# Token sums moved to VectorE, transposes half a tile later, one load and some weight work reordered

## The reference, cut to what matters

```
hp = hp + mix_out(a_p, d_p, w_out)                                  # 1024 x 1024
hp = hp + swiglu(rms_norm(hp, norm_ffn_g), w_gate, w_up, w_down)    # D_FF = 2816
y  = rms_norm(hp, final_norm_g)

def swiglu(h, w_gate, w_up, w_down):
    g = einsum('bsd,df->bsf', h, w_gate)
    u = einsum('bsd,df->bsf', h, w_up)
    return einsum('bsf,fd->bsd', silu(g) * u, w_down)
```

## Time and profile before

| | |
|---|---|
| median of three runs | 2763.15 us |
| the profiled execution | 2758.85 us, span 2757.0 us |
| TensorE busy | 2566.0 us (93%) |
| VectorE busy | 1827.6 us (66%) |
| ScalarE busy | 1211.1 us (44%) |
| GpSimd busy | 602.7 us (22%) |

### The profile page before, as it was taken

One profiled execution on the slowest core, in us unless ns is written; L12 is line 12 of the kernel. 1 busy time (PEld: TensorE's weight loads), 2 busy tenths in 40 slices (PEclk: granted clock), 3 DMA queues, 4 the chain that ended last, 5 costly groups with the idle time before them and its releaser, 6 DMA issues.

```text
span 2757.0 us, 48148 instructions
## 1 busy us (share of the span) xinstructions
PE 2566.0 (93%) x19292; PEld 1592.7 (58%) x19292; DVE 1827.6 (66%) x3577; ACT 1211.1 (44%) x2108; POOL 602.7 (22%) x610
## 2 busy tenths in 40 slices
PE   3999999978899998887899999999889999999998
PEld 1666666656677766443344444444447777766666
DVE  8777776668878773666787788776554444444445
ACT  4566666657889997443232233223331111111112
POOL 1211111105667666122312111201120000000001
PEclk9999999988999999998999999999999999999999
DMA  5123211142210000523353334434212222222222
GB/s 183 56 73 107 95 59 66 46 110 49 40 32 9 9 9 9 191 108 138 130 184 115 115 133 175 151 122 149 105 39 69 70 79 87 88 77 69 70 74 76
DMA packets 149872, 245.81 MB, mean 89 GB/s; under 512 B 47298, under 2 KB 102002, under 8 KB 148114
## 3 DMA queue, kind: packets, MB, share of 16 engines
q1 hardware_dynamic: 149650, 242.74, 26.6%
HBM read 148.83 MB, written 90.94 MB: 87 GB/s over the span
## 4 chain that ended last, share of the span: by engine, by line
PE 50%; DVE 3%; issue 2%; POOL 2%; DMA 1%; ACT 1%; SPq 0%; POOLq 0%; DVEq 0%; ACTq 0%
PE bank L2843 10%; PE bank L2844 10%; PE bank L2845 10%; PE bank L2858 6%; PE bank L2860 5%; PE bank L2859 5%; PE bank L2795 1%; PE bank L2796 1%; PE bank L2797 1%; DMA tail_buffers<-mix_scratch 1%; PE bank L2778 1%; DVE tail_buffers L2216 1%; ACT tail_buffers L2567 0%; POOL tail_buffers L2102 0%; DMA out_y_prompt<-residual_rows 0%
## 5 line engine op out<-in xcount | busy, mean ns | idle before, releaser
L2843 PE MATMUL bank<-ffn_inT_sums,tail_buffers 128*128 128x512 f16 (+2 forms) x1848 | 579.8, 314 | 5.5 <-ACT tail_buffers L2605 3.0
L2844 PE MATMUL bank<-ffn_inT_sums,tail_buffers 128*128 128x512 f16 (+2 forms) x1848 | 579.4, 314 | 0.0
L2845 PE MATMUL bank<-ffn_inT_sums,tail_buffers 128*128 128x512 f16 (+2 forms) x1848 | 579.4, 314 | 0.0
L2342 DVE SCALAR_TENSOR_TENSOR residual_rows<-bank,pair_scales,residual_rows 128x512 f32<-128x512 f32 (+1 forms) x374 | 273.1, 747 | 114.7 <-PE bank L2860 114.3
L2858 PE MATMUL bank<-tail_buffers 128*128 128x512 f16 (+1 forms) x748 | 286.9, 384 | 20.3 <-issue 10.2
L1095 PE MATMUL z_ps<-w_in_hi_lo,normT_hi 128*128 128x384 f16 x816 | 268.4, 329 | 21.7 <-DVE w_in_hi_lo L682 21.7
L2859 PE MATMUL bank<-tail_buffers 128*128 128x512 f16 (+1 forms) x748 | 286.3, 383 | 0.0
L2860 PE MATMUL bank<-tail_buffers 128*128 128x512 f16 (+1 forms) x748 | 286.3, 383 | 0.0
L1096 PE MATMUL z_ps<-w_in_hi_lo,normT_hi 128*128 128x384 f16 x816 | 268.5, 329 | 0.0
L1097 PE MATMUL z_ps<-w_in_hi_lo,normT_lo 128*128 128x384 f16 x816 | 268.2, 329 | 0.0
L2843 PEld LDWEIGHTS bank<-ffn_inT_sums,tail_buffers 128*128 128x128 f16 x1848 | 181.3, 98 | 105.8 <-issue 5.6
(11 more groups left out here) (333 smaller groups left out, 5151.0 us busy)
## 6 DMA issues: line engine op xcount, KB each, us to landing
gate_up_scratch<-tail_buffers SPq DMA_DIRECT2D x77, 512.0 KB, 3.2
tail_buffers<-gate_up_scratch SPq DMA_DIRECT2D x77, 512.0 KB, 3.5
tail_buffers<-in_w_gate SPq DMA_DIRECT2D x22, 512.0 KB, 5.4
tail_buffers<-in_w_up SPq DMA_DIRECT2D x22, 512.0 KB, 6.5
tail_buffers<-in_w_down SPq DMA_DIRECT2D x22, 512.0 KB, 5.9
down_scratch<-tail_buffers SPq DMA_DIRECT2D x22, 512.0 KB, 3.1
tail_buffers<-down_scratch SPq DMA_DIRECT2D x22, 512.0 KB, 4.4
keys_values<-in_w_in SPq DMA_DIRECT2D x8, 1152.0 KB, 16.0
```

The source lines that it names most:

```text
L2342: nc.vector.scalar_tensor_tensor(out, BK[y_bank(e, y)][0:rows, :], PS[0:rows, i, F_YI:F_YI + 1], out, ALU.mult, ALU.add).then_inc(h_ok, 1)
L2843: nc.tensor.matmul(out, wh, nh, start=first and k == 0, stop=False, skip_group_check=True)
L2844: nc.tensor.matmul(out, wh, nl, start=False, stop=False, skip_group_check=True)
L2845: last = nc.tensor.matmul(out, wl, nh, start=False, stop=k == 3, skip_group_check=True)
```

## The change

1. The four differences of a unit are made by VectorE, in the tile in which the unit's second row is normalised, right behind `norm_row`; their order is now 0, 1, 2, 3.
2. The split of the 2048 columns is cut in two (`row_hi` and `row_lo` with m = 2 and 3), the second behind the tile's last batch of copies.
3. Every batch of transposes comes one half product later. Batch 0 of unit 3 stands in the middle of the second half product of tile 8; its batches 1 to 3, and batch 3 of unit 7 besides all of unit 8, stand between the first products of the FFN.
4. `load_mix(Q0 + 2)` (the third tile of the second half) is issued ahead of the last two loads of residual rows and of the loads of stored weights.
5. In pairs 0 and 1 of the first half, maxima, scales and slots of the next pair come earlier on VectorE and ScalarE, and slots 5 and 6 of pair 1 come later, at the start of pair 1.

```diff
 def turn_at(q, n):
-    u, m = norm_unit(q)
-    if q == 8:
-        return 3, n
-    if u in (0,):
+    k = 2 * q + n - 5 if q < Q0 else 2 * (q - Q0) + n + 15
+    if k < 0 or k == 15:
         return None
-    return (4 if u == 5 else u - 1), 2 * m + n
+    return k // 4, k % 4
...
+                load_mix(Q0 + 2)
                 load_rows(Q0 + 6)
                 load_rows(Q0 + 7)
                 for j in range(3):
                     slot_back(0, j)
                 down_back(0)
-                for q in range(Q0 + 2, NTT):
+                for q in range(Q0 + 3, NTT):
                     load_mix(q)
...
-                def token_sums(u):      # on GpSimd
...
+                def token_sums(u):      # on VectorE
...
+                    nc.vector.tensor_tensor(part(0), NF[1][:, half[0]], NF[0][:, half[0]], ALU.subtract).then_inc(t_ok, 1)
+                    dve.wait_ge(t_ok, 4 * u + 1)
+                    nc.vector.tensor_tensor(part(1), NF[1][:, half[1]], part(0), ALU.subtract).then_inc(t_ok, 1)
+                    nc.vector.tensor_tensor(part(2), NF[1][:, half[1]], NF[1][:, half[0]], ALU.subtract).then_inc(t_ok, 1)
+                    dve.wait_ge(t_ok, 4 * u + 2)
+                    nc.vector.tensor_tensor(part(3), NF[0][:, half[1]], part(1), ALU.subtract).then_inc(t_ok, 1)
...
# output_tile(q) on VectorE
                     elif q:
                         norm_row(q - 1)
+                        if norm_unit(q - 1)[1]:
+                            token_sums(norm_unit(q - 1)[0])
                         row_lo(*norm_unit(q - 1))
                     residual(q, 0)
...
+                    both = 4 if q == Q0 else norm_unit(q - 1)[0] if q and norm_unit(q - 1)[1] else None
+                    if both is not None:
+                        row_lo(both, 2)
+                    if q == Q0 - 1:
+                        turned_lo(3, 0)
                     residual(q, 1)
-                    if turn_at(q, 1):
+                    if turn_at(q, 1) and q != Q0 - 1:
                         turned_lo(*turn_at(q, 1))
+                    if both is not None:
+                        row_lo(both, 3)
...
# pairs 0 and 1 on VectorE, first half
+                    if i == 1:
+                        slot_lo(1, 5)
+                        slot_lo(1, 6)
                     if i:
                         max_down(i)
+                    if i == 1:
+                        max_gate_up(2, 0)
                     product_act(0, i, i, 512, 0)
...
+                    if i == 1:
+                        max_gate_up(2, 1)
                     sum_2(0, i, 512, 1)
...
+                    if i == 0:
+                        max_gate_up(1, 0)
                     if i == 1:
-                        max_gate_up(2, 0)
+                        gate_up_scales(2)
                     sum_3(0, i, 512, 0)
...
                     if i == 1:
-                        max_gate_up(2, 1)
+                        slot_lo(2, 0)
                     sum_3(0, i, 512, 1)
...
                     if i == 0:
-                        max_gate_up(1, 0)
+                        max_gate_up(1, 1)
                     product_act(0, i, i, 512, 1)
...
-                    slots_at = {2: 0, 4: 1, 6: 2, 8: 3, 10: 4, 12: 5, 14: 6} if i == 0 else {1: 3, 3: 4, 5: 5, 7: 6} if i == 1 else {1: 6}
+                    slots_at = {1: 0, 3: 1, 6: 2, 9: 3, 12: 4} if i == 0 else {1: 3, 3: 4, 5: 5, 7: 6} if i == 1 else {1: 6}
...
# the middle of the last tile's second half product on TensorE
                     for m in range(2):
+                        if q == Q0 - 1 and n == 1 and m == 1:
+                            turn(3, 0)
```

More of the change, by code:

```diff
@@ L2443, in _ @@
                         down_lo(0, 0)
-                    if i == 1:
-                        gate_up_scales(2)
-                        slot_lo(2, 0)
                     block_21(0, i, 512, 1)
-                    if steady:
-                        slot_lo(i + 1, 4)
-                    if i == 0:
+                    if i:
+                        if more:
+                            slot_lo(i + 1, 4 if steady else 1)
+                    else:
                         down_lo(0, 1)
                     product_act(0, i, i, 512, 2)
[L2453 to L2456, removed]
                     block_12(0, i, 512, 0)
                     act_lo(0, 0, i, 512, 2)
[L2459 to L2462, removed]
+                    if i and more:
+                        slot_lo(i + 1, 5 if steady else 2)
+                    if i == 0:
+                        gate_up_scales(1)
                     block_12(0, i, 512, 1)
@@ L2487, in _ @@
                 norm_row(NTT - 1)
+                token_sums(8)
                 row_lo(8, 1)
@@ L2564, in row_hi @@
                     if u:
-                        act.wait_ge(tn_ok, 4 * (u - 1) + (1, 2, 4)[m])
-                    c, x = ((slice(0, 1024), NF[0]), (slice(1024, 1536), NF[1][:, half[1]]), (slice(1536, 3584), TC[e]))[m]
+                        act.wait_ge(tn_ok, 4 * (u - 1) + m + 1)
+                    c, x = ((slice(0, 1024), NF[0]), (slice(1024, 1536), NF[1][:, half[1]]),
+                            (slice(1536, 2560), TC[e][:, 0:1024]), (slice(2560, 3584), TC[e][:, 1024:2048]))[m]
                     nc.scalar.activation(NHL[e][0][:, c], x, ACT.Copy).then_inc(xh_ok, 1)
@@ L2651, in output_tile @@
                         turned_hi(*turn_at(q, 0))
-                    if q == Q0:
-                        row_hi(4, 2)
-                    elif q and norm_unit(q - 1)[1]:
-                        row_hi(norm_unit(q - 1)[0], 2)
+                    both = 4 if q == Q0 else norm_unit(q - 1)[0] if q and norm_unit(q - 1)[1] else None
+                    if both is not None:
+                        row_hi(both, 2)
+                    if q == Q0 - 1:
+                        turned_hi(3, 0)
                     squares_out(q)
-                    if turn_at(q, 1):
+                    if turn_at(q, 1) and q != Q0 - 1:
                         turned_hi(*turn_at(q, 1))
+                    if both is not None:
+                        row_hi(both, 3)
                 mix_hi(0)
@@ L2697, in _ @@
                         slot_hi(i + 1, 2)
+                    if i == 1:
+                        slot_hi(2, 0)
                     silu(0, i, i, 512, 1)
@@ L2904, in _ @@
                             gate_up(0, i, 0, i, j, x)
-                            if i == 0 and j < 2 and x == (1, 0)[j]:
-                                turn(3, 2 + j)
+                            if i == 0 and (j, x) in ((0, 1), (1, 0), (1, 1)):
+                                turn(3, 1 + j + (x if j else 0))
                     pe.wait_ge(d_lo, 2 * i + 2)
@@ L2924, in _ @@
                                 gate_up(1, i, b, n, j, x)
+                                if i == 0 and b == 0 and (j, x) == (0, 0):
+                                    turn(7, 3)
                                 if i == 0 and b == 0 and (j, x) in ((1, 1), (5, 1), (6, 0), (6, 1)):
```

72 lines of the change are left out of this document (30 added, 42 removed).

## The result

The changed kernel takes 2716.27 us, the median of four runs (2713.87 to 2721.05), against 2762.63 (2759.69 to 2764.78): the ratio is 0.9835, with a 95% interval from 0.9817 to 0.9853. The forecast was 2720.6 in a range of 2704 to 2742. A repeat in a later batch (e0_after) gave 2715.61 and 0.9841 [0.9823, 0.9858].

The account below looks back on a forecast made before the run. TensorE's waits and the slow clock behind them bound the three changed windows; gains of 6 + 7.5 + 8.5 + 10.5 + 10 = 42.5 us off 2763.15 gave 2720.6 us, range 2704 to 2742.

Parts of the forecast that it names:

- Unit by unit: Two-tile unit: old 3.9 us transposes wait goes, about 2.4 comes at mixer rows; 29.4 us instead of 31.1.
- The clock term: Slow TensorE clock behind the new mixer-row wait of about 2.4 us: up to 1.6 us, taken as 1.2.
- rival (a): Tile units and pairs 0, 1: 2.4 us waits don't lower the clock; 11 us more gained, 2709; chance 0.17.
- The load: Mixer rows of tile 11, loaded earlier: TensorE's wait falls from 9.1 to 2 us; 10.5 us gained.
- Units 5 to 7: Second projection stage: 31.1, 32.7 and 37.1 us become 29.4, 29.4 and 32.3; 10 us gained.
- Pair 1: Earlier maxima, scales and slots cut the 10.2 us wait before down products to 1.7 to 3; 8.5 gained.
- Pair 0: Down products: earlier maximum cuts 4.7 us wait to 2.5, removes 3.8; sums' overlap costs 1 to 1.5; gain 7.5.
- (b): Tiles gain nothing because VectorE and ScalarE in series set the pace; unit stays 31 us; about 2730; chance 0.17.
- (d): VectorE's differences take 2.23 us each under contention; 51 us more in eight units; 2772; chance 0.02.
- (e): The moves don't come about because another semaphore holds the same place; about no change; chance 0.02.
- (c): Weight work of pairs 0 and 1 gains half, since reductions, sums and VectorE collide; 8 us less, 2729; chance 0.10.

Follow-up runs that it names:

- e2: Parts 1 to 3 in the kernel before, with load and pairs left as they were: 2735.58 us, ratio 0.9908.
- e4: Changed kernel with the four differences back on GpSimd in their new order, all else kept: 2711.14 us, ratio 0.9814.
- e5: Changed kernel with five one-column two-tensor scale instructions written with the second column as scalar operand: 2715.36 us, ratio 0.9831.
- e6: Changed kernel with pair 0's scales for the second unit put back behind the cast of the activations: 2715.98 us, ratio 0.9836.
- e12: Changed kernel with GpSimd's weight sums of pairs 1 and 2 delayed until VectorE has cast the activations of the pair before: 2719.94 us.
- The three parts alone: Kernel before with only the load moved, only the tile stages changed, or only pairs 0 and 1 reordered: 2746.81, 2735.58 and 2752.37 us.
- e10: Changed kernel with differences on GpSimd except unit 4's, one-input scale columns, tile 8's copies first, first maxima behind tiles 3 and 5: 2704.16 us.
- e11: e10 with the delay of GpSimd's weight sums from e12: 2707.97 us, ratio 0.9806.
- e7_copy_first: Changed kernel with tile 8's copies of unit 2's last batch ahead of norm_row on VectorE and the split on ScalarE: 2715.59 us.

## Why the prediction was right, and where it was not

- **Unit by unit (right).** The series of VectorE and ScalarE was worked out row by row and came out within 0.1 us (the lo half of the mixer rows is over at 21.1 in the unit that begins at 1959.65, forecast 21.2). The wait moved to the mixer rows, 4.0 in tile 5 (forecast 4 to 5) and 6.1 in tile 8 (forecast 6). e2 shows that it is parts 1 to 3 that give it, and e4 that parts 2 and 3 do it without part 1.
- **The clock term (too dear).** The wait at mixer rows was set at 2.4 with 1.2 of slow clock behind it. It is 1.7 to 1.8 in the units that repeat in the second half, since TensorE itself comes half a microsecond later, and nothing behind these waits is slow: the mean clock of the stage is 1.00. A unit takes 28.4 there, not 29.4. So the gain of rival (a)'s first half came in this stage, but its condition, that a wait of 2.4 leaves the clock alone, was not met by these shorter waits. The one wait of 2.3 (tile 3) went both ways: 0.67 for 3.5 us behind it here, 1.00 in e0_after.
- **The load (right).** The sum had 10.5 with a wait of 2 left. Between e2 and the changed kernel it gives 10.3, and a wait of 1.5 is left; in the kernel before, where VectorE's series is shorter there, none is left and it gives 12.9.
- **Units 5 to 7 (too low).** So the 5.5 us more in this stage are theirs: 15.7 (e2) where 10 was forecast. The largest piece is the last unit: from the transposes of tile 16's mixer rows to the end of the stage the trace went from 52.4 to 45.1, 7.4 less, where the working had 37.1 to 32.3 up to the FFN's fourth product, 4.8 less.
- **Pair 1 (right).** 9.5 against 8.5. The wait of 10.2 is 2.4, inside the forecast 1.7 to 3.
- **Pair 0 (the step that failed).** The first half of the sum held: the wait of 4.7 is 2.7 (forecast 2.5). The second did not: "the 3.8 us wait goes" and "the sums now overlap VectorE's two-input work at the start of the down products, costing 1 to 1.5 us". The sums began where they were forecast (0.5 us ahead of the down products), but the price of the overlap is some 7 us: in these rows each VectorE instruction with two operands from SBUF that starts beside a sum pays 1.3 to 2.2, whether it has 512 columns or one. The step priced wide instructions at the down products only; the scales, sixteen small instructions of which four have two operands, are no term of it. e5 took their surplus away (2.3 to 3.1 of it came back), e6 showed that it passes to whatever else stands there, and e12 that pair 0 takes 56.0 when the sums wait: 1.0 from the 54.95 of the forecast (62.45 - 7.5).
- **Rivals.** (b), (d) and (e) are out: the unit fell, a difference takes 0.69, not 2.23, and the time moved. (c) is half true, in pair 0 only: reductions and sums collide there. The Trainium skill (SBUF — State Buffer, Who interferes with whom) has the rule in full: VectorE with two SBUF inputs and GpSimd reading SBUF block each other for a whole instruction, VectorE with one input doesn't outside its two-port modes, and a cast can enter such a mode. The rows agree, also where the working forgot it: 2.30 for two columns as tensors, 0.21 with one of them as a scalar operand, 1.75 for the cast of four columns.
- **What stays open.** The three parts alone add up to 2.0 us more than the whole does. The medians don't tell it from noise, but the traces have 2.6 of overlap between the load and the tiles in the second projection stage, of which the wait of 1.5 is a part. The medians fell by 46.4 and the profiled executions by 40.3; the traces explain the latter. Why the profiled executions differ by up to 5.5 us ahead of tile 3 was not looked into beyond the clock of tile 1. A delay of the sums in pair 0 only would give e10 the 2.6 that e11 gains there; that is an estimate, and no kernel shows it.

## What to carry to other kernels

Before an instruction chain is moved, look at what the other engine does at its new time, and count every two-input instruction that falls beside it, the one-column ones too: here each paid up to a whole instruction of the other side. Before work is moved off a late engine, see whether the consumer can simply come later: here that kept the wait away with the work left where it was (e4), and the move only lengthened the series that was then late. And where two errors can cancel in a sum, check the terms by place, not the total.

## What the runs showed of the hardware that was not expected

- A VectorE instruction on 128x1 took 1.7 to 2.3 us beside GpSimd's 128x1024 sums and 0.15 alone. The adds to the residual, with one operand from a bank, took 0.69 each (2.06 for three at 1309.53 in e12) beside the sums: unaffected. The sum beside the slots took 3.33 instead of 2.34 (1305.19 in e12), so both sides pay.
- Passing the second column as the scalar operand cost 0.21 and was not blocked.
- Between a GpSimd partition reduction and the next weight sum lie 6.95 us in pair 0 and 7.14 in pair 1 of the changed kernel, 7.18 and 6.78 in pair 0 of e5 and e6, and 8.73 before the change, with nothing that the profile shows as a cause.
- TensorE's clock, in the changed kernel: after waits of 1.5, 1.7 and 1.8 us the transposes ran at the full rate (1.07 for sixteen); after 4.01 and 6.1 at the low level (1.89 and 1.86). Between these the length of the wait alone does not tell: after the wait of 2.3 in tile 3 the granted clock was 0.67 for 3.5 us in one execution, 1.00 in another (e0_after) and 0.50 for 2.9 us in e7_copy_first.
